# Rotary partners by DMA and in-place rotation inside the last recurrent head, convolution spread out, in a two-layer hybrid trunk

## Chip, core and metric

One NeuronCore of a Trainium2 chip runs the whole program. The metric is the device time of one execution, in microseconds (us).

## What is computed

Two layers over 288 tokens (256 of a new prompt, 8 times 4 of running samples). Each layer projects the normalised input to 40 tiles of 128 columns, feeds three mixers from them (windowed attention with sinks, HGRN2 recurrence, short gated convolution), projects their outputs back, and adds a SwiGLU block. The change is about the rotary embedding of queries and keys and about when the convolution runs:

```python
def partial_rope(x, pos):          # the first 16 of 64 dimensions of a head
    x1, x2 = xr[..., :half], xr[..., half:]                     # half = 8
    rot = jnp.concatenate([x1 * cos - x2 * sin, x2 * cos + x1 * sin], axis=-1)
    return jnp.concatenate([rot, x[..., ROT_DIM:]], axis=-1)

def short_conv(u, buf, w):         # u = cc * ch; the result is multiplied by cb
    up = jnp.concatenate([buf, u], axis=1)
    y = w[0] * up[:, 0:L] + w[1] * up[:, 1:1 + L] + w[2] * up[:, 2:2 + L]
```

The first eight dimensions of a head and the next eight are each other's partners. Row `d` of a tile needs its own value times cos plus its partner's value times sin with a sign.

## The kernel before

**Layout.** Features lie on the 128 partitions, tokens on the free axis. All weights stream from HBM as 754 slabs of 512 KB. SP loads a slab into one of four buffers `raw`, ACT rounds it (`hi`, L417, `whi`), DVE makes the remainder (`lo`, L712, `wlo`), and PE multiplies with both (L1459 to L1461: `whi` with the high and the low part of the activations, `wlo` with the high part). One slab is 2 tiles by 4 chunks by 3, that is 24 matmuls of 128x288. ACT and DVE work two slabs ahead of PE (`LEAD`); a buffer comes free when PE is through with its slab.

**Fill-in work.** The mixers run in the gaps of this stream. On each engine a mixer is a Python generator; after each slab (on PE in the recurrent heads after each half slab) every engine takes the generator's next step and runs on to the next `yield`. So the order of each engine's queue is set by where the `yield`s stand, and an engine that waits inside a step holds up the slabs behind it.

**Order of a layer.** The projection makes the tiles of the recurrence first (0 to 15: `HQ`, `HF`, `HI`, `HG`), then queries (16 to 23, `Q0`), keys and values (24, 25 and 26, 27, `KV`), and last the convolution's (28 to 39, `CB`, `CC`, `CH`). Four recurrent heads (`hgrn`, 8 slabs each) fill the time while tiles 16 to 31 are made, so tiles 16 to 27 are ready at the end of the third head. Then come two halves of attention (`attn`, `gg` = 0 and 1), 16 slabs each: `gg` = 0 beside the last projection slabs, `gg` = 1 beside the first half of the output projection. `conv` runs beside `gg` = 1; the second half of the output projection waits for its end (`half_b`).

**Head 3 on DVE.** Its generator ends with: `near` (the last masked copy, L829), a step in which heads 0 to 2 open the next head and head 3 does nothing, `sample_state(0)` (L898, waits for PE's `out`), then reciprocal, scaling and gating of the output (L905, L907, L911, after ACT's square root), `sample_state(1)` (L898), and the remainder `ml` (L916, after ACT's `mh`, L491). `hgrn_over` makes an engine wait for the ends of all these before it starts attention.

**Rotary before.** At the head of each half PE multiplies five tiles (one key tile, four query tiles) by a signed permutation, `partners` (L1602: four after the first slab, one after the second). DVE multiplies by sin (L973), POOL multiplies the tile by cos (L1349), DVE adds (L977) into `krg` or `qg`. ACT makes `krx`, the key tile with its halves swapped (L543, L544), and copies the sample queries to `qs` (L552). PE's first scores, `score(0)` (L1614), come after the third slab. POOL also copies the values (`vst_a`, L1351). `conv` starts at its sixth step and takes one piece per step to its thirteenth.

## Time and profile before

| | |
|---|---|
| median of 3 runs | 2590.35 us (2590.34 to 2590.42) |
| the profiled execution's own time | 2590.64 us |
| its span in the trace | 2588.9 us, 51434 instructions |
| TensorE | 99% busy, 19400 matmuls |
| VectorE, ScalarE, GpSimd | 57%, 39%, 14% busy |
| DMA | 419.97 MB, mean 162 GB/s |

The span runs from the first to the last recorded instruction; the execution's own time has 1.7 us around it. Busy times of matmuls overlap, because they are pipelined: the distance of two starts tells what one costs. In a timeline row the columns are start, duration, engine, line, operation, tiles and count, and in brackets the engine's idle time before it with what ended it.

### The profile page before, as it was taken

What the parts mean: (1) busy time and instruction counts of PE and PEld (TensorE: products, weight loads), DVE (VectorE), ACT (ScalarE), POOL (GpSimd) and SP (SyncE); (2) the same over time, 40 slices, a digit from 0 to 9 for tenths busy, and PEclk for the clock granted to TensorE, in tenths of its full rate; (3) what the DMA queues carried; (4) which work ended last, traced back from release to release, by engine and by line L of the source; (5) the groups of instructions that cost most, each with busy time, mean ns of one, the idle gap of its engine ahead of it and who ended that gap; (6) DMA issues with size and microseconds to landing.
All of it is one profiled execution on the core that took longest, in us unless ns stands there. A gap on an engine that the chain in (4) does not pass through costs nothing.

```text
span 2588.9 us, 51434 instructions
## 1 busy us (share of the span) xinstructions
PE 2558.7 (99%) x19400; PEld 2519.2 (97%) x19400; DVE 1483.5 (57%) x2055; ACT 1013.7 (39%) x1401; POOL 349.8 (14%) x290
## 2 busy tenths in 40 slices
PE   8999999999999999999999999999999999999997
PEld 8999999999999999999999999999999999999997
DVE  5576797555544445555545767875555444555455
ACT  5344554333333333333334544543333333333333
POOL 2001113111110011111100121031111000111111
PEclk9999999999999999999999999999999999999998
DMA  6544444444445444544454544445454455444443
GB/s 223 164 153 163 159 143 146 166 166 163 168 164 170 164 164 161 168 162 163 162 163 163 174 150 142 145 155 178 161 171 159 165 163 161 162 162 162 170 163 126
DMA packets 115724, 419.97 MB, mean 162 GB/s; under 512 B 13376, under 2 KB 14656, under 8 KB 115584
## 3 DMA queue, kind: packets, MB, share of 16 engines
q1 hardware_dynamic: 109152, 397.72, 45.9%
q0 software_dynamic: 3472, 14.04, 1.5%
q10 hardware_dynamic: 3024, 7.16, 0.7%
q8 instruction: 52, 0.85, 0.1%
q14 instruction: 24, 0.20, 0.0%
HBM read 411.06 MB, written 11.87 MB: 163 GB/s over the span
## 4 chain that ended last, share of the span: by engine, by line
PE 97%; DVE 1%; POOL 1%; ACT 0%; issue 0%; DMA 0%; SPq 0%; DVEq 0%; POOLq 0%; ACTq 0%
PE gp L1459 31%; PE gp L1461 30%; PE gp L1460 30%; PE mb L1503 1%; PE mb L1614 1%; PE mb L1635 0%; PE mb L1627 0%; POOL acc L1387 0%; PE mb L1602 0%; PE mb L1573 0%; DVE rstd L737 0%; DVE wlo L712 0%; DMA raw<-wstream 0%; PE mb L1512 0%; DVE x L1262 0%
## 5 line engine op out<-in xcount | busy, mean ns | idle before, releaser
L1459 PE MATMUL gp<-xh,whi 128*128 128x288 f32 x4096 | 1225.7, 299 | 12.6 <-DVE xl L1147 9.7
L1460 PE MATMUL gp<-xl,whi 128*128 128x288 f32 x4096 | 1209.7, 295 | 0.0
L1461 PE MATMUL gp<-xh,wlo 128*128 128x288 f32 x4096 | 1205.7, 294 | 0.0
L712 DVE TENSOR_TENSOR wlo<-raw,whi 128x1024 fp32r<-128x1024 f32 x754 | 970.9, 1321 | 336.4 <-ACT whi L417 332.5
L417 ACT ACTIVATE whi<-raw 128x1024 fp32r<-128x1024 f32 x754 | 769.1, 1052 | 572.3 <-PE gp L1461 541.9
L1459 PEld LDWEIGHTS gp<-xh,whi 128*128 128x128 f32 x4096 | 769.1, 188 | 24.7 <-issue 23.6
L1461 PEld LDWEIGHTS gp<-xh,wlo 128*128 128x128 f32 x4096 | 772.4, 189 | 0.0
L1460 PEld LDWEIGHTS gp<-xl,whi 128*128 128x128 f32 x4096 | 770.5, 188 | 0.8
L1459 PE MATMUL gp<-fh,whi 128*128 128x288 f32 x1408 | 416.7, 296 | 0.0
L1460 PE MATMUL gp<-fl,whi 128*128 128x288 f32 x1408 | 415.4, 295 | 0.0
L1461 PE MATMUL gp<-fh,wlo 128*128 128x288 f32 x1408 | 414.0, 294 | 0.0
L1461 PEld LDWEIGHTS gp<-fh,wlo 128*128 128x128 f32 x1408 | 265.2, 188 | 0.0
L1460 PEld LDWEIGHTS gp<-fl,whi 128*128 128x128 f32 x1408 | 264.3, 188 | 0.0
L1459 PEld LDWEIGHTS gp<-fh,whi 128*128 128x128 f32 x1408 | 263.8, 187 | 0.0
L1419 POOL TENSOR_TENSOR gw<-gb,gs 128x576 f32<-128x576 f32 x44 | 63.3, 1439 | 1246.1 <-ACT gs L604 1246.1
L608 ACT ACTIVATE fh<-fa 128x576 f32 (+1 forms) x44 | 30.2, 685 | 284.8 <-DVE fa L1111 284.8
L1111 DVE TENSOR_TENSOR fa<-gp,gw 128x288 f32<-128x288 f32 x88 | 36.2, 453 | 177.7 <-PE gp L1461 177.7
L1105 DVE TENSOR_TENSOR gb<-gp,rstd 128x288 f32<-128x288 f32 x88 | 36.2, 452 | 171.7 <-PE gp L1461 171.4
L604 ACT ACTIVATE gs<-gb 128x576 f32<-128x576 f32 x44 | 30.2, 686 | 263.6 <-DVE gb L1105 263.6
L752 DVE TENSOR_TENSOR x<-gp,x 128x288 f32 (+1 forms) x128 | 52.3, 450 | 138.4 <-PE gp L1461 138.3
L1421 POOL TENSOR_TENSOR gw<-gw,rstd 128x576 f32<-128x576 f32 x44 | 100.9, 2293 | 3.4
L424 ACT ACTIVATE xh<-x,par x64 | 30.8, 529 | 167.5 <-DVE x L752 167.5
(251 smaller groups left out, 1881.7 us busy)
## 6 DMA issues: line engine op xcount, KB each, us to landing
raw<-wstream SPq DMA_DIRECT2D x754, 512.0 KB, 4.2
s<-s_cache POOLq DMA_DIRECT2D x8, 512.0 KB, 9.7
hs_out<-s ACTq DMA_DIRECT2D x8, 512.0 KB, 2.8
caches_out<-caches POOLq DMA_DIRECT2D x8, 496.0 KB, 7.8
x<-x_in ACTq DMA_DIRECT2D x4, 576.0 KB, 8.5
y_out<-x SPq DMA_DIRECT2D x4, 576.0 KB, 2.8
kct<-kt_cache POOLq DMA_DIRECT2D x4, 512.0 KB, 6.3
vct<-v_cache POOLq DMA_DIRECT2D x4, 512.0 KB, 7.2
```

Of the source, the lines that this page charges most:

```text
L417: a.activation(whi[slot][:], raw[slot][:], ACT.Copy).then_inc(hi_ready, 1)
L424: m = a.activation(xh[:, bass.ds(2 * j + c, 1), :], x[:, bass.ds(2 * j + c, 1), :], ACT.Copy, scale=pcol(P_GAIN, tn * KC + 2 * j + c))
L604: a.activation(gs[:], gb[:], ACT.Sigmoid).then_inc(sig_ready, 1)
L712: v.tensor_tensor(wlo[slot][:], raw[slot][:], whi[slot][:].bitcast(F32), ALU.subtract).then_inc(lo_ready, 1)
L752: m = v.tensor_tensor(xc, gp[2 * bank + c][:, 0:TOK], xc, ALU.add)
L1105: m = v.tensor_tensor(gb[:, c, :], gp[c][:, 0:TOK], rstd[:], ALU.mult)
L1111: m = v.tensor_tensor(fa[:, c, :], gp[2 + c][:, 0:TOK], gw[:, c, :], ALU.mult)
L1419: e.tensor_tensor(gw[:], gb[:], gs[:], ALU.mult).then_inc(gw_steps, 1)
L1421: e.tensor_tensor(gw[:], gw[:], rstd[:].unsqueeze(1).to_broadcast([P, 2, TOK]), ALU.mult).then_inc(gw_steps, 1)
L1459: t.matmul(out, w_hi, mv_hi, start=first, stop=False)
L1460: t.matmul(out, w_hi, mv_lo, start=False, stop=False)
L1461: mm = t.matmul(out, w_lo, mv_hi, start=False, stop=last)
```

## The change

- **POOL**, after the recurrent heads, issues four DMAs (`rotary_partners`) that copy the partner rows of tiles 16 to 27, 8 partitions each, into rows of tiles that heads 0 to 2 are through with (`partner`, tiles 0 to 2, 4 to 6, 8 to 10, 12 to 14). Its cos products, the copy of the values and their waits go; the stores read `pj` itself.
- **DVE**, in head 3's empty step, multiplies all ten partner tiles by a signed sin and all ten tiles by cos in place (`rotary_products`: 2592, 288 and 2880 elements a partition). Behind `sample_state(0)` it adds the two (`rotary_sum`: 2592 and 288). This serves both halves. The sign is put into sin once, at the start.
- **PE** loses the `partners` matmuls. `score(0)` moves from the third step of a half to the first, and all that follows moves up by two steps.
- **ACT** makes `krx` in the first step instead of the second; the copies to `qs` move behind the first `turned`.
- **conv** on DVE takes its pieces at steps 2, 4, 6, 8, 10, 12 and 14 instead of 6 to 11 and 13; its buffers move out of the way of the hidden tiles.

```diff
-ROPE_ORDER = (4, 0, 1, 2, 3)
+ROTATED = KV + 2 - Q0
...
+        rot_sign = sb("rot_sign", [P, 1])
...
-        over = [wide[0] + size([P, Q0, TOK]), wide[0] + size([P, CB, TOK])]
+        over = [wide[0] + size([P, HI + 3, TOK]), wide[0] + size([P, HG, TOK])]
+        krx = sub(over, "krx", [P, TOK])
...
+        assert tail[1] == temp[0]
+        over = [tail[0], temp[1]]
+        up = sub(over, "up", [P, 4, UPW])
+        yc = sub(over, "yc", [P, 4, UPW - 2])
+        t = [over[0], temp[1]]
...
+        partner = pj[:, 0:Q0, :].rearrange("p (a b) t -> p a b t", b=4)[:, :, 0:3, :]
...
-                for _ in range(6):
+                for _ in range(3):
...
-                for _ in range(5):
+                for _ in range(9):
...
+                a.wait_ge(rv.sem, rv.at(l, "rot"))
+                a.activation(krx[0:64, :], pj[64:128, KV + gg, :], ACT.Copy)
+                a.activation(krx[64:128, :], pj[0:64, KV + gg, :], ACT.Copy).then_inc(aa.sem, aa.step("krx"))
...
                 for u in range(3):
                     turned(u)
+                    if u == 0:
+                        queries()
                     yield
...
+                    v.tensor_reduce(rot_sign[:], rot, AX.X, ALU.add)
...
+                    v.tensor_scalar(sin, sin, rot_sign[:, 0:1], -1.0, ALU.mult, ALU.mult)
...
+            def rotary_products(l):
+
+                v.wait_ge(group_out, attn_in(l))
+                v.wait_ge(partners_loaded, l * 64 + 64)
+                v.tensor_tensor(partner[:, 0:3], partner[:, 0:3], sin.unsqueeze(1).unsqueeze(1).to_broadcast([P, 3, 3, TOK]),
+                                ALU.mult)
+                v.tensor_tensor(partner[:, 3, 0, :], partner[:, 3, 0, :], sin, ALU.mult).then_inc(rv.sem, rv.step("sin"))
+                v.tensor_tensor(pj[:, Q0:Q0 + ROTATED, :], pj[:, Q0:Q0 + ROTATED, :],
+                                cos.unsqueeze(1).to_broadcast([P, ROTATED, TOK]), ALU.mult).then_inc(rv.sem, rv.step("cos"))
+
+            def rotary_sum(l):
+                v.wait_ge(rv.sem, rv.at(l, "cos"))
+                nine = pj[:, Q0:Q0 + 9, :].rearrange("p (a b) t -> p a b t", b=3)
+                v.tensor_tensor(nine, nine, partner[:, 0:3], ALU.add)
+                v.tensor_tensor(pj[:, Q0 + 9, :], pj[:, Q0 + 9, :], partner[:, 3, 0, :], ALU.add
+                                ).then_inc(rv.sem, rv.step("rot"))
...
                 if not last:
                     opening(T + 1, h + 1)
+                else:
+                    rotary_products(l)
                 yield
...
                 sample_state(0, "ssa", 1)
+                if last:
+                    rotary_sum(l)
                 yield
...
-                for _ in range(5):
-                    yield
-
-                v.wait_ge(at.sem, at.at(T * 2 + 1, "R3"))
-                v.wait_ge(ap_.sem, ap_.at(T * 2 + 1, "vst"))
+                yield
+                v.wait_ge(group_out, conv_in(T))
...
-                for n in ROPE_ORDER[:4]:
-                    rope(n)
-                yield
-                rope(ROPE_ORDER[4])
...
+            def rotary_partners(l):
+
+                T = l * HG_HEADS + HG_HEADS - 1
+                e.wait_ge(group_out, attn_in(l))
+                e.wait_ge(ho.sem, ho.at(T, "q"))
+                e.wait_ge(hs.sem, hs.at(T, "sig_g"))
+                e.wait_ge(hp.sem, hp.at(T, "gate"))
+                apart(e)
+                rows, half = pj[:, Q0:CB, :].rearrange("p (a b) t -> p a b t", b=3), ROT_DIM // 2
+                for head in (0, HEAD_DIM):
+                    for to, of in ((head, head + half), (head + half, head)):
+                        e.dma_start(partner[to:to + half], rows[of:of + half]).then_inc(partners_loaded, 16)
...
-                for k, n in enumerate(ROPE_ORDER):
-                    if k >= 2:
-                        e.wait_ge(av.sem, av.at(T, f"rot{ROPE_ORDER[k - 2]}"))
-                    tile = 4 * gg + Q0 + n if n < 4 else gg + KV
-                    apart(e)
-                    e.tensor_tensor(rt_a[:, k % 2, :], pj[:, bass.ds(tile, 1), :].rearrange("p o t -> p (o t)"), cos,
-                                    ALU.mult).then_inc(ap_.sem, ap_.step(f"cos{n}"))
-                e.tensor_copy(vst_a[:], pj[:, bass.ds(gg + (KV + 2), 1), :].rearrange("p o t -> p (o t)")
-                              ).then_inc(ap_.sem, ap_.step("vst"))
...
-                e.wait_ge(av.sem, av.at(T, f"rot{ROPE_ORDER[-1]}"))
+                e.wait_ge(rv.sem, rv.at(l, "rot"))
...
                     hgrn(l * HG_HEADS + h, h, l)
+                rotary_partners(l)
                 for gg in range(2):
...
-                    t.wait_ge(av.sem, av.at(T, f"sc{u - 1}" if u else "rot3"))
-                    if u == 0:
+                    if u:
+                        t.wait_ge(av.sem, av.at(T, f"sc{u - 1}"))
+                    else:
+                        t.wait_ge(rv.sem, rv.at(l, "rot"))
...
-                            keys = krg if i == u // 2 else krx
-                            mm = t.matmul(mb[i][:, m_ * P:(2 * m_ + 1) * P], qg[rows, u, m_ * P:(m_ + 1) * P],
+                            keys = pj[:, KV + gg, :] if i == u // 2 else krx
+                            mm = t.matmul(mb[i][:, m_ * P:(2 * m_ + 1) * P], pj[rows, Q0 + 4 * gg + u, m_ * P:(m_ + 1) * P],
...
-                for n in ROPE_ORDER[:4]:
-                    partners(n)
-                yield
-                t.wait_ge(av.sem, av.at(T, f"sin{ROPE_ORDER[0]}"))
-                partners(ROPE_ORDER[4])
-                yield
                 score(0)```

VectorE's queue from the end of `near` in head 3 to the end of the head, before the change (`wlo` is a slab's remainder, `s` the sample state, `pj` the projected tiles):

```order
L829 COPY_PREDICATED AT<-half_mask_60,mb 128x2x4x16
L712 TENSOR_TENSOR wlo_85<-raw_77,whi_81 128x1024
L898 SCALAR_TENSOR_TENSOR s_118<-s_118,tot,mb 128x128 x4
L712 TENSOR_TENSOR wlo_82<-raw_74,whi_78 128x1024
L905 RECIPROCAL osq<-osq 128x288
L907 SCALAR_TENSOR_TENSOR osb<-osb,par,osq 128x288
L911 TENSOR_TENSOR osb<-osb,gate 128x288
L898 SCALAR_TENSOR_TENSOR s_118<-s_118,tot,mb 128x128 x4
L712 TENSOR_TENSOR wlo_83<-raw_75,whi_79 128x1024
L916 TENSOR_TENSOR ml<-osb,mh 128x288
```

The same piece of VectorE's queue with the change:

```order
L849 COPY_PREDICATED AT<-half_mask_61,mb 128x2x4x16
L713 TENSOR_TENSOR wlo_86<-raw_78,whi_82 128x1024
L786 TENSOR_TENSOR pj<-pj,cst 128x3x864
L788 TENSOR_TENSOR pj<-pj,cst 128x288
L789 TENSOR_TENSOR pj<-pj,cst 128x2880
L920 SCALAR_TENSOR_TENSOR s_116<-s_116,tot,mb 128x128 x4
L795 TENSOR_TENSOR pj<-pj 128x2592
L796 TENSOR_TENSOR pj<-pj 128x288
L713 TENSOR_TENSOR wlo_83<-raw_75,whi_79 128x1024
L929 RECIPROCAL osq<-osq 128x288
L931 SCALAR_TENSOR_TENSOR osb<-osb,par,osq 128x288
L935 TENSOR_TENSOR osb<-osb,gate 128x288
```

The three products stand ahead of the state update, the two sums between it and the remainder of the first slab of attention; the reciprocal and all behind it follow.

ScalarE's queue from the head's end to the first steps of attention, before the change:

```order
L491 ACTIVATE mh<-osb 128x288 [waits hgrn_vector]
L494 DMA hp_out<-s_117 128x128 [waits hgrn_scalar]
L496 DMA hs_out<-s_118 128x1024 [waits hgrn_vector]
L417 ACTIVATE whi_80<-raw_76 128x1024 [waits slab_used,raw_ready2]
L417 ACTIVATE whi_81<-raw_77 128x1024 [waits hgrn_gpsimd,hgrn_sigmoids,hgrn_tensor,hgrn_scalar,hgrn_opening,hgrn_vector,slab_used,raw_ready3,attn_vector]
L543 ACTIVATE krx<-krg 64x288 [waits attn_vector]
```

and with the change:

```order
L490 ACTIVATE mh<-osb 128x288 [waits hgrn_vector]
L493 DMA hp_out<-s_115 128x128 [waits hgrn_scalar]
L495 DMA hs_out<-s_116 128x1024 [waits hgrn_vector]
L416 ACTIVATE whi_81<-raw_77 128x1024 [waits slab_used,raw_ready2]
L552 ACTIVATE krx<-pj 64x288 [waits hgrn_gpsimd,hgrn_sigmoids,hgrn_tensor,hgrn_scalar,hgrn_opening,hgrn_vector,rotary_vector,attn_vector]
L553 ACTIVATE krx<-pj 64x288
```

The swapped key tile is now made ahead of the second `whi` of attention, straight behind the wait for the whole recurrence.

## Rows read from the trace of the kernel before

**Rows 1.** List of PE's waits, whole span (engine, line, releaser: us, times, longest).
```profile
PE gp L1459 <- DVE xl L1147: 9.7, 1, 9.7
PE mb L1493 <- POOL acc L1288: 3.9, 1, 3.9
PE gp L1459 <- DVE wlo L712: 2.3, 4, 0.8
PE mb L1614 <- DVE qg L977: 0.8, 2, 0.4
```

**Rows 2.** PE's timeline around the first four partner matmuls of layer 0.
```profile
254.71 0.30 PE L1460 MATMUL gp<-xl,whi 128*128 128x288 f32 x1
...
260.84 0.29 PE L1461 MATMUL gp<-xh,wlo 128*128 128x288 f32 x1
260.98 2.10 PE L1602 MATMUL mb<-pj,cst 128*128 128x288 f32 x8
...
263.05 0.30 PE L1460 MATMUL gp<-xl,whi 128*128 128x288 f32 x1
```

**Rows 3.** PE's groups of instructions by shape (count, busy us, mean ns).
```profile
L1602 PE MATMUL mb<-pj,cst 128*128 128x288 f32 x40 | 11.0, 405 | 0.0
```

**Rows 4.** DVE's timeline at the end of head 3 of layer 0.
```profile
242.39 1.22 DVE L712 TENSOR_TENSOR wlo<-raw,whi 128x1024 fp32r<-128x1024 f32 x1
252.61 1.12 DVE L898 SCALAR_TENSOR_TENSOR s<-s,tot,mb 128x128 f32<-128x128 f32 x4 [9.00 <-PE mb L1582]
253.65 1.22 DVE L712 TENSOR_TENSOR wlo<-raw,whi 128x1024 fp32r<-128x1024 f32 x1
255.31 1.95 DVE L905 RECIPROCAL osq<-osq 128x288 f32<-128x288 f32 x1 [0.44 <-ACT osq L487]
...
259.26 1.22 DVE L712 TENSOR_TENSOR wlo<-raw,whi 128x1024 fp32r<-128x1024 f32 x1
260.40 0.45 DVE L916 TENSOR_TENSOR ml<-osb,mh 128x288 fp32r<-128x288 f32 x1
```

**Rows 5.** The same timeline in layer 1, the state update of head 3.
```profile
1530.20 1.12 DVE L898 SCALAR_TENSOR_TENSOR s<-s,tot,mb 128x128 f32<-128x128 f32 x4 [9.01 <-PE mb L1582]
```

**Rows 6.** DVE's groups by shape, window of the second half, layer 0.
```profile
L964 DVE TENSOR_TENSOR al<-pj,ah 128x1152 fp32r<-128x1152 f32 x1 | 1.4, 1354 | 0.0
```

**Rows 7.** POOL's timeline in head 3 of layer 0.
```profile
229.38 0.55 POOL L1303 DMA_DIRECT2D s<-s_cache  x1
...
232.69 2.28 POOL L1314 TENSOR_TENSOR vm<-vks,own 96x512 f32<-96x512 f32 x1 [1.11 <-ACT vks L448]
```

**Rows 8.** The profile's DMA queue and DMA issues (count, KB each, us to landing).
```profile
q1 hardware_dynamic: 109152, 397.72, 45.9%
...
s<-s_cache POOLq DMA_DIRECT2D x8, 512.0 KB, 9.7
...
cv_out<-cnew POOLq DMA_DIRECT2D x2, 36.0 KB, 2.8
```

**Rows 9.** ACT's timeline at the start of attention, layer 0.
```profile
259.83 2.27 ACT L417 ACTIVATE whi<-raw 128x1024 fp32r<-128x1024 f32 x2 [0.95 <-DVE s L898]
264.20 0.44 ACT L543 ACTIVATE krx<-krg 64x288 f32<-64x288 f32 x1 [2.11 <-DVE krg L977]
264.66 0.44 ACT L544 ACTIVATE krx<-krg 64x288 f32<-64x288 f32 x1
```

**Rows 10.** PE's timeline at the span's start and end.
```profile
9.68 0.58 PE L1459 MATMUL gp<-xh,whi 128*128 128x288 f32 x1 [9.68 <-DVE xl L1147]
...
15.82 0.32 PE L1460 MATMUL gp<-xl,whi 128*128 128x288 f32 x1
...
2569.58 0.29 PE L1461 MATMUL gp<-fh,wlo 128*128 128x288 f32 x1
2573.81 1.33 PE L1493 MATMUL mb<-acc,mean_x 128*128 128x288 f32 x2 [3.94 <-POOL acc L1288]
```

**Rows 11.** Busy time in the stretch 2572 to 2573 (PE, PEld, DVE, ACT, POOL, granted clock, DMA share, GB/s).
```profile
2572.00:2573.00 1.00, 0.00 (x0) 0.00 (x0) 0.68 (x1) 0.98 (x2) 0.92 (x2) 0.72 0.00 0
```

More of the change, by code:

```diff
@@ L535, in turned, with queries @@
                     m.then_inc(aa.sem, aa.step(f"pT{u}"))
+                def queries():
+                    a.wait_ge(ap_.sem, ap_.at(T, "qs0"))
+                    for g in range(2):
+                        for i in range(4):
+                            half = 64 * (i % 2)
+                            at_ = 16 * g + DEC_SEQ * i
+                            m = a.activation(qs[64 * g:64 * g + 64, :, at_:at_ + DEC_SEQ], pj[half:half + 64, Q0 + 4 * gg + 2 * g + i // 2, SEQ:TOK]
+                                             .rearrange("p (b t) -> p b t", t=DEC_SEQ), ACT.Copy)
+                    m.then_inc(aa.sem, aa.step("qs"))
                 def out_hi(u):
@@ L1597, in attn @@
                 t.wait_ge(aa.sem, aa.before(T))
-                def partners(n):
-                    tile = 4 * gg + Q0 + n if n < 4 else gg + KV
-                    t.matmul(mb[ROPE_ORDER.index(n) % 4][:, 0:TOK], rot, pj[:, bass.ds(tile, 1), :].rearrange("p o t -> p (o t)"),
-                             start=True, stop=True).then_inc(at.sem, at.step(f"R{n}"))
                 def score(u):
-                    t.wait_ge(av.sem, av.at(T, f"sc{u - 1}" if u else "rot3"))
-                    if u == 0:
+                    if u:
+                        t.wait_ge(av.sem, av.at(T, f"sc{u - 1}"))
+                    else:
+                        t.wait_ge(rv.sem, rv.at(l, "rot"))
                         t.wait_ge(aa.sem, aa.at(T, "krx"))
@@ L1673, in attn @@
                                 at_ = 2 * P + r * SAMP
-                                mm = t.matmul(mb[0][rows, at_:at_ + SAMP], qs[:, b, :], krg[:, SEQ:TOK],
+                                mm = t.matmul(mb[0][rows, at_:at_ + SAMP], qs[:, b, :], pj[:, KV + gg, SEQ:TOK],
                                               start=True, stop=True)
```

77 lines of the change are left out of this document (22 added, 55 removed), and 1 row of the table av.

## The prediction

> **What bounds the kernel now.** I began with the list of PE's waits, since PE is busy for nearly the whole span: PE waits about 17 us in 2588.9, and 13.6 of them lie at the program's two ends, where this change does nothing [rows 1]. So time is gained only by taking instructions off PE or by ending one of its few waits, and it is lost wherever a new wait opens. In the part that changes, the list has one entry: the first scores of an attention half wait for DVE's rotated queries, 0.8 us in two pieces of 0.4 [rows 1]. Then I read PE's timeline where the permutation matmuls stand, for what one costs between its neighbours [rows 2], and last the queues of DVE, POOL and ACT around the end of head 3, because the work goes there [rows 4, 7, 9].
>
> **What comes off PE.** The neighbours of the first four permutation matmuls are 47 matmuls of the stream whose first and last start 6.13 us apart, so one costs 6.13 / 46 = 0.133 us [rows 2]. From the start of the last of them at 260.84 to the start of the second matmul behind the permutations at 263.05 there are 2.21 us, where two steps of 0.133 would stand: four permutations cost 2.21 - 0.27 = 1.94 us, or 0.485 each. The trace has 40 records for them, two for each (8 records for these four) [rows 2, 3]: 20 matmuls, 20 x 0.485 = **9.7 us**. Nothing covers them, PE being the bound. The old wait before the scores, **0.8 us**, goes with them.
>
> **Three products on DVE.** Two rows give the price by size: 288 elements take 0.45 us [rows 4], 1152 take 1.354 [rows 6], so 1.046 ns an element. 2592 elements come to 2.86 us and 2880 to 3.16; an instruction starts some 0.08 before the one ahead of it ends (a remainder of 1.22 us begins 1.14 before its follower, [rows 4]). The products take 2.78 + 0.37 + 3.08 = 6.2 us. They are covered: DVE is idle for 9.0 us, from 243.6 until PE's `out` releases the state update at 252.6, in layer 1 as well [rows 4, 5]. They end at 249.8 with 2.8 us to spare. If that cover were gone, each us would go to the chain below.
>
> **The four DMAs.** POOL ends head 3's last product at 234.97 and has nothing else; an issue takes 0.55 [rows 7], so the last is out at 237.2. How long an SBUF-to-SBUF copy of 8 partitions takes, the trace doesn't show. Bounds: 2.8 us, a 36 KB store alone on the queue, and 9.7 us, a 512 KB load behind another [rows 8]; 108 KB four times lies between, and I take 6, landing at 243.2, just before DVE asks. What lands before 246.4 costs nothing. At the upper end, 246.9, it is 0.5 us a layer.
>
> **The two sums on DVE, the costly part.** They stand behind the state update and ahead of the first remainder of attention: 2.78 + 0.37 = 3.15 us, where DVE has no idle time to speak of. Followed through the old rows: the remainder starts at 253.65 + 3.15 = 256.8 and ends at 258.0. PE wants it at 257.8 (24 steps of 0.133 before 260.98, [rows 2]), so PE waits **0.3 us**. The reciprocal starts at 257.9 instead of 255.31 (it had waited 0.44 for ACT), 2.6 later, and `ml` ends at 260.85 + 2.6 = 263.5 [rows 4]. What waits for `ml`: ACT, before it swaps the key tile. Its store waits for the second state update and its next `whi` starts at 259.83 + 2.6 = 262.4, ending at 263.5 [rows 9]; then the two half copies, 0.46 + 0.44, so `krx` is there at 264.5. And PE now asks for its first scores after one slab, not three. That slab starts 0.3 late, at 258.1, and PE is at the scores at 261.35. **A new wait of 264.55 - 261.35 = 3.2 us**, in each layer. The second half's scores need only a key swap ahead of which the first half has ended two steps sooner: no wait.
>
> Bounds of this wait: if the sums took half as long, the remainder would be in time and the wait 1.6; if they took twice as long, it would be 6.3 and the remainder 3.4 late. I take the row's price, since the operands are of the same kind.
>
> **The rest.** POOL loses its cos products and the copy of the values, which PE never waited for. The copies to `qs` move behind the first transposes and delay the second exponentials; PE's list has no wait for any exponential so far [rows 1], and if their slack were too short, it would show there. The convolution issues the same instructions, spread out; no entry of PE's list names any of them, before or at its end [rows 1], so it is worth nothing, and if DVE fell behind there it would show as a wait of the third or fourth transposes, tenths of a us. The sign of sin costs two small DVE instructions once, ahead of remainders; all of PE's waits for remainders are four, 2.3 us [rows 1], and two such instructions could add some 0.5.
>
> **The sum.** -9.7 - 0.8 + 2 x 0.3 + 2 x 3.2 = -3.5 us against the profiled execution (2590.64, that is the span of 2588.9 and 1.7 around it). The median of the runs is 0.3 lower; from it, 2586.85.
>
> **The clock.** One cost remains that the sum leaves out. When PE stands still long enough, its granted clock falls. After the last stream matmul (started 2569.58) PE had nothing to do, and the stretch 2572 to 2573 has a mean of 0.72 granted, that is a fall from 2.4 to 1.2 GHz at about 2572.4, 2.5 us into the standstill [rows 10, 11]. At the start, after 9.7 us without work, 25 matmuls stand 0.24 us apart, from 9.68 to 15.82, where 0.133 would do [rows 10]: 6.14 - 3.33 = 2.8 us lost. A new wait of 3.2 us is longer than the 2.5 and may set off the same. Bounds: nothing, or 2.8 in both layers, 5.6. I take 2.0, one fall of a shorter kind, since the standstill is a third as long as that at the start. Then the time is 2590.35 - 3.5 + 2.0 = **2588.8**.
>
> The Trainium skill has a rule that speaks against this change: in "TensorE: Matmul & The Clock Gate", section "Why this matters for your kernels", idle gaps between bursts of matmuls are to be avoided because an idle stretch brings the array back to half rate. The trace agrees that it happens, with the fall at 2572.4. By that rule in full the kernel would take 2592.4, without it 2586.85.
>
> **Rivals.**
> 1. *The new wait is short or absent* (0.20). For it: the chain runs through four engines' queues, and a guess of 0.5 us too much at three places brings the wait to 1.7; the stated price of the sums could be too high. Against: in the changed order of ACT, `krx` waits for the whole recurrence. Without the wait -9.7 - 0.8 + 0.6 = -9.9, 2580.4; with 1.6 us and no late remainder 2583.0.
> 2. *The partners come late and DVE stands in its queue for them* (0.08). All of DVE's later work, `out`'s consumers and the remainders, is behind that wait. A copy touches only 8 partitions, so its rows may go to few of the 16 DMA engines. The stream's packets took 0.459 x 16 x 2588.9 / 109152 = 0.174 us each at 3.6 KB [rows 8]. The partners are 128 runs of 3.4 KB, some 21 us on one engine, 2.7 on eight. On one they land near 259, 12.7 us late, twice: 2586.85 + 25.4 = **2612**, slower. It decides from a landing at 248.2 on (the gain of 3.5 is gone), and over 0.2% from 250.8. For it: no row shows such a copy. Against: 512 KB take 9.7 us even behind another load.
> 3. *The clock falls in both layers and stays down long, and the wait is a little longer than 3.2* (0.12): 2592.4 to 2597.
> 4. That the change does not do what it says: PE's changed list has no permutation left, so this can't be more than a trifle.
>
> **How the numbers follow.** A run tells about 0.2%, 5.2 us, from no change: faster means under 2585.2, slower over 2595.5. My forecast, a wait of 2.4 to 4 us with no, one or two falls of the clock, has 0.60 and lies between 2585.5 and 2593, inside the bound. Rival 1 (0.20) gives faster, and 0.02 of the forecast's lower edge too. Rival 2 (0.08) is mostly slower; half of rival 3 (0.06) is. So faster 0.22, same 0.65, slower 0.13. For 8 in 10 the range takes the forecast, the upper half of rival 1 and most of rival 3: 2582.5 to 2595.
>
> **What would show it.** PE's wait list should have the first scores (L1619) twice, near 3.2 us, released by ACT's `krx`, and the first remainder of attention for 0.3; no row of permutations; the sums at 2.8 us each layer, right behind the state update; DVE's idle time before that update down to about 2.8 us. If the granted clock falls, matmuls behind the wait stand 0.24 us apart. The prediction is wrong if the scores wait under 1 us, if the products wait for the DMAs beyond 246.4, or if PE waits in the second half of attention, where the spread convolution stands.

## The result, and the profile after

| | |
|---|---|
| before, median | 2590.35 us |
| changed, median of 20 runs | **2596.24 us** (2588.53 to 2600.11) |
| ratio to before | 1.0019, 95% interval 1.0012 to 1.0025 |
| forecast | 2588.8 us, range 2582.5 to 2595.0 |

The change made the kernel 5.9 us slower, and its median lies 1.2 us above the upper end of the range. The scatter is new too: the runs of the kernel before lie within 0.9 us, those of the changed kernel over 11.6 us. The profiled execution happened to be the fastest of them, 2588.53 us. Its list of TensorE's (PE's) waits (engine, line, what ended the wait: us, times, longest):

```profile
PE gp L1468 <- DVE xl L1157: 9.6, 1, 9.6
PE mb L1619 <- ACT krx L553: 6.1, 2, 3.1
PE mb L1502 <- POOL acc L1298: 3.9, 1, 3.9
PE gp L1468 <- DVE wlo L713: 2.4, 5, 0.8
...
PE mb L1575 <- ACT vks L471: 0.4, 1, 0.4
```

Beside [rows 1] the wait of the scores for the rotated queries (0.8) is gone, and the new wait of the first scores for `krx` is there: 6.1 us in two pieces. The last row is new too, and it is the small end of what cost most. The same kernel's PE timeline at the standstill:

```profile
257.34 0.29 PE L1470 MATMUL gp<-xh,wlo 128*128 128x288 f32 x1
257.86 0.37 PE L1468 MATMUL gp<-xh,whi 128*128 128x288 f32 x1 [0.23 <-DVE wlo L713]
...
260.99 0.29 PE L1470 MATMUL gp<-xh,wlo 128*128 128x288 f32 x1
264.35 0.55 PE L1619 MATMUL mb<-pj 64*128 64x128 f32 x1 [3.07 <-ACT krx L553]
...
266.34 0.44 PE L1469 MATMUL gp<-xl,whi 128*128 128x288 f32 x1
266.58 0.44 PE L1470 MATMUL gp<-xh,wlo 128*128 128x288 f32 x1
```

No matmul starts between 260.99 and 264.35; behind it the stream's matmuls stand 0.24 us apart instead of 0.133. The granted clock had fallen to 1.2 GHz: over 264 to 268 its mean is 0.57 (stretch; busy time of PE, PEld, DVE, ACT, POOL, then granted clock, DMA share, GB/s), while the same place of layer 1 shows no fall behind the same standstill.

```profile
264.00:268.00 4.00, 3.65 (x18) 3.03 (x19) 2.83 (x5) 2.55 (x3) 3.12 (x7) 0.57 0.83 279
...
1542.00:1546.00 4.00, 4.00 (x32) 3.67 (x33) 3.45 (x9) 2.38 (x3) 3.52 (x7) 1.00 0.88 293
```

A mean of 0.57 over 4 us is 4 x 0.43 / 0.5 = 3.4 us at 1.2 GHz, at most 1.7 us lost. DVE's timeline beside [rows 4]:

```profile
244.75 2.86 DVE L786 TENSOR_TENSOR pj<-pj,cst 128x2592 f32<-128x2592 f32 x1 [0.21 <-DMA pj<-pj]
...
247.90 3.15 DVE L789 TENSOR_TENSOR pj<-pj,cst 128x2880 f32<-128x2880 f32 x1
252.31 1.12 DVE L920 SCALAR_TENSOR_TENSOR s<-s,tot,mb 128x128 f32<-128x128 f32 x4 [1.27 <-PE mb L1591]
253.35 2.85 DVE L795 TENSOR_TENSOR pj<-pj 128x2592 f32<-128x2592 f32 x1
256.12 0.45 DVE L796 TENSOR_TENSOR pj<-pj 128x288 f32<-128x288 f32 x1
256.49 1.22 DVE L713 TENSOR_TENSOR wlo<-raw,whi 128x1024 fp32r<-128x1024 f32 x1
257.63 1.94 DVE L929 RECIPROCAL osq<-osq 128x288 f32<-128x288 f32 x1
```

Sums, late remainder and reciprocal stand where the prediction put them, within 0.4 us. The products start 1.2 us later than it said (244.75 in place of 243.6, the last 0.2 for the DMAs) and end with 1.27 us to spare in place of 2.8. What the prediction left out is ScalarE's (ACT's) queue a little earlier. First the kernel before, then the changed one, from `whi` to the copies of the turned keys (`vks`), for which PE's next state product waits:

```profile
239.13 1.06 ACT L417 ACTIVATE whi<-raw 128x1024 fp32r<-128x1024 f32 x1 [5.93 <-DMA raw<-wstream]
240.70 1.06 ACT L417 ACTIVATE whi<-raw 128x1024 fp32r<-128x1024 f32 x1 [0.52 <-DMA raw<-wstream]
243.09 1.06 ACT L417 ACTIVATE whi<-raw 128x1024 fp32r<-128x1024 f32 x1 [1.32 <-PE gp L1461]
...
246.06 0.27 ACT L472 ACTIVATE vks<-mb 96x128 f32<-96x128 f32 x1
```

```profile
237.94 1.06 ACT L416 ACTIVATE whi<-raw 128x1024 fp32r<-128x1024 f32 x1 [5.69 <-DMA raw<-wstream]
242.23 1.06 ACT L416 ACTIVATE whi<-raw 128x1024 fp32r<-128x1024 f32 x1 [3.23 <-DMA raw<-wstream]
245.08 1.06 ACT L416 ACTIVATE whi<-raw 128x1024 fp32r<-128x1024 f32 x1 [1.79 <-DMA raw<-wstream]
...
247.07 0.27 ACT L471 ACTIVATE vks<-mb 96x128 f32<-96x128 f32 x1
```

In the kernel before, ACT already waited for DMA ahead of two of the three slabs, and ahead of the third for PE alone. In the changed kernel it waits for DMA ahead of all three, the third starts 2 us later, and the key copies stand behind it in ACT's queue. The DMA view of 229 to 246 (issues: count, KB each, median us to landing) has the reason; again before, then changed:

```profile
raw<-wstream SPq DMA_DIRECT2D x6, 512.0 KB, 7.0
```

```profile
raw<-wstream SPq DMA_DIRECT2D x5, 512.0 KB, 9.7
pj<-pj POOLq DMA_DIRECT2D x4, 108.0 KB, 6.0
```

The partner copies themselves land after 6.0 us in the median, the value I had taken. But the weight slabs beside them land after 9.7 us instead of 7.0.

### The profile page after: what moved, and what is told of

Same layout as the page of the kernel before. It is cut to its first block and busy times, and to the rows that moved or that the text cites. A ratio compares the mean times of both kernels' runs of the same rounds, so it can differ in the third digit from the quotient of the medians.

```text
span 2586.9 us, 51267 instructions
## 1 busy us (share of the span) xinstructions
PE 2550.8 (99%) x19360; PEld 2512.3 (97%) x19360; DVE 1483.0 (57%) x2027; ACT 1012.0 (39%) x1401; POOL 327.2 (13%) x274
## 3 DMA queue, kind: packets, MB, share of 16 engines
q1 hardware_dynamic: 109152, 397.72, 46.2%
## 5 line engine op out<-in xcount | busy, mean ns | idle before, releaser
L1468 PE MATMUL gp<-xh,whi 128*128 128x288 f32 x4096 | 1225.4, 299 | 12.6 <-DVE xl L1157 9.6
L1469 PE MATMUL gp<-xl,whi 128*128 128x288 f32 x4096 | 1209.8, 295 | 0.0
L1470 PE MATMUL gp<-xh,wlo 128*128 128x288 f32 x4096 | 1205.7, 294 | 0.0
L713 DVE TENSOR_TENSOR wlo<-raw,whi 128x1024 fp32r<-128x1024 f32 x754 | 969.6, 1320 | 338.4 <-ACT whi L416 334.6
L416 ACT ACTIVATE whi<-raw 128x1024 fp32r<-128x1024 f32 x754 | 769.0, 1052 | 584.3 <-PE gp L1470 545.0
L1468 PEld LDWEIGHTS gp<-xh,whi 128*128 128x128 f32 x4096 | 769.2, 188 | 25.2 <-issue 24.3
L1470 PEld LDWEIGHTS gp<-xh,wlo 128*128 128x128 f32 x4096 | 772.5, 189 | 0.0
L1469 PEld LDWEIGHTS gp<-xl,whi 128*128 128x128 f32 x4096 | 770.6, 188 | 0.6
L1468 PE MATMUL gp<-fh,whi 128*128 128x288 f32 x1408 | 416.7, 296 | 0.0
L1469 PE MATMUL gp<-fl,whi 128*128 128x288 f32 x1408 | 415.4, 295 | 0.0
L1470 PE MATMUL gp<-fh,wlo 128*128 128x288 f32 x1408 | 414.0, 294 | 0.0
L1470 PEld LDWEIGHTS gp<-fh,wlo 128*128 128x128 f32 x1408 | 265.2, 188 | 0.0
L1469 PEld LDWEIGHTS gp<-fl,whi 128*128 128x128 f32 x1408 | 264.3, 188 | 0.0
L1468 PEld LDWEIGHTS gp<-fh,whi 128*128 128x128 f32 x1408 | 263.8, 187 | 0.0
## 6 DMA issues: line engine op xcount, KB each, us to landing
raw<-wstream SPq DMA_DIRECT2D x754, 512.0 KB, 4.2
s<-s_cache POOLq DMA_DIRECT2D x8, 512.0 KB, 9.7
hs_out<-s ACTq DMA_DIRECT2D x8, 512.0 KB, 2.8
kct<-kt_cache POOLq DMA_DIRECT2D x4, 512.0 KB, 4.9
vct<-v_cache POOLq DMA_DIRECT2D x4, 512.0 KB, 6.4
```

The costliest lines, as they stand in the source:

```text
L416: a.activation(whi[slot][:], raw[slot][:], ACT.Copy).then_inc(hi_ready, 1)
L713: v.tensor_tensor(wlo[slot][:], raw[slot][:], whi[slot][:].bitcast(F32), ALU.subtract).then_inc(lo_ready, 1)
L1468: t.matmul(out, w_hi, mv_hi, start=first, stop=False)
L1469: t.matmul(out, w_hi, mv_lo, start=False, stop=False)
L1470: mm = t.matmul(out, w_lo, mv_hi, start=False, stop=last)
```

## The experiments

The lines ahead of each result are what was put down before the run. All medians are of 5 to 11 executions; those of the kernel before on the same chips were 2590.3 to 2590.6. In kernels with an edit the line numbers stand a few lines off.

**The same kernel again.** No edit.

> The changed kernel once more, for a second profiled execution. Its 20 runs lay between 2588.5 and 2600.1 us, far wider than the 0.9 us of the kernel before, and the profiled one was the fastest. Theory A (clock): TensorE stands still for about 3.3 us before the first scores of each layer, the granted clock falls after some of these standstills and not after others, and each fall costs several us because it stays at 1.2 GHz longer than the 3.4 us that the fastest run shows. So a slower execution shows one or two longer stretches at 1.2 GHz that begin just behind the standstills (near 264 and 1541 us), and its excess over 2588 us is about half of their length; the wait itself stays at 3.1 us. Theory B (transfers): the partners land at another time in each execution, so a slower execution shows the wait before the first scores itself longer, by the excess, with the vector engine waiting for the transfers. Theory C (second half): the excess lies in waits behind 265 us that the spread convolution makes. Median 2594 to 2598 us by all three.

Measured 2596.0 us (2590.08 to 2603.4). The profiled execution took 2591.35 and shows both things: the score wait unchanged at 2 x 3.1, a mean clock below one behind both standstills (3.4 us at 1.2 GHz each), and a wait for the key copies of 2.0 us:

```profile
PE mb L1619 <- ACT krx L553: 6.1, 2, 3.1
...
PE mb L1575 <- ACT vks L471: 2.0, 2, 1.3
```

Theory B as I had put it (partners late, score wait longer) has nothing for it: that wait is 6.1 in both profiles of this kernel. Neither profile is of one of the longer executions, though.

**Filling the wait.** In `attn` on PE, `gg` = 0:

```diff
-                    t.wait_ge(hv.sem, hv.last(l * HG_HEADS + HG_HEADS, "ssb"))
                     t.wait_ge(ha.sem, ha.last(l * HG_HEADS + HG_HEADS, "root"))
+                    for _ in range(6):
+                        t.matmul(mb[3][:, 0:TOK], rot, cos, start=True, stop=True)
+                    t.wait_ge(hv.sem, hv.last(l * HG_HEADS + HG_HEADS, "ssb"))
```

> Only edit: six products of the rotation matrix with the cosines (128x288 floats, about 0.49 us each, 2.9 us together, into a bank that is read by nobody) run on TensorE in the wait before the first scores of each layer. The wait for the rotated tiles is then nearly as long as before but the engine works in it. Theory A: the granted clock does not fall there, so the runs draw together to within about 1 us and the median is about 2587 us (the sum without the clock, 2586.85). Theories B and C: the spread stays 8 to 12 us wide and the median stays at 2595 to 2597 us.

Measured 2593.11 us (2587.71 to 2596.88). That is 2.9 us less with useless work in the wait. With scatters of 13 and 9 us this pair alone doesn't prove A; the same pair without copies, further down, does (3.6 us, scatters of 2.4 and 1.2). The spread stayed at 9 us and the median 6 us above A's 2587, so A is not all. The profiled execution has no fall of the clock behind the score place and waits 2.7 us at L1575 in one layer.

**Attention two slabs later.** Two empty steps (`if gg == 0: yield; yield`) ahead of the first scores on PE and DVE and behind `krx` on ACT; on PE:

```diff
+                if gg == 0:
+                    for _ in range(2):
+                        yield
                 score(0)
                 yield
```

> Only edit: in the first half the attention of all three engines starts two slabs later (two empty steps ahead of the first scores on TensorE, VectorE and ScalarE), as it stood in the kernel before. The rotated tiles are ready when the scores come. Theory A: no standstill, so no fall of the clock: 2586.85 less the 6.4 us of the two waits, about 2580.5 us, runs within 1 us of each other. Theory B: the transfers land as late as before but nobody waits for them so soon: about 2580.5 us too, but VectorE still waits for them in some executions. Theory C: the spread of 8 to 12 us stays, about 2590 us.

Measured 2590.74 us (2588.62 to 2595.41). The score wait is gone and 5.3 us are gained, where A and B gave 15. Two rows of PE's waits say what took its place:

```profile
PE gp L1474 <- DVE wlo L716: 6.4, 8, 1.7
...
PE mb L1581 <- ACT vks L471: 2.3, 2, 1.7
```

DVE's sums stand ahead of remainders, and without the score wait PE stands for such a remainder, 1.7 us in each layer; and the key copies are late here too. So one wait was hidden behind the other. Behind the wait of 1.7 us for the key copies, in layer 0, the clock fell as well: its mean over 250 to 262 is 0.86, that is 12 x 0.14 / 0.5 = 3.4 us at 1.2 GHz.

**Half the sums.** `rotary_sum(l, 0)` adds the five tiles of the first half in head 3; `rotary_sum(l, 1)` the other five in attention, behind `out_lo(0)`; the second half's users wait for the second sum.

```diff
-                v.tensor_tensor(nine, nine, partner[:, 0:3], ALU.add)
...
+                for to, p in (((0, 3), partner[:, 0]), ((3, 4), partner[:, 1, 0:1]), ((8, 9), partner[:, 2, 2:3])
+                              ) if gg == 0 else (((4, 6), partner[:, 1, 1:3]), ((6, 8), partner[:, 2, 0:2]),
+                                                 ((9, 10), partner[:, 3, 0:1])):
+                    tiles = pj[:, Q0 + to[0]:Q0 + to[1], :]
+                    m = v.tensor_tensor(tiles, tiles, p, ALU.add)
+                m.then_inc(rv.sem, rv.step("rot1" if gg else "rot"))
```

> Only edit: the sum of the rotary products is made for the five tiles of the first half in the last recurrent head (about 1.65 us in place of 3.3) and for the other five tiles four steps later, in the attention of the first half. The wait before the first scores gets shorter by about 1.65 us, to some 1.5 us. Theory A: the standstill is half as long, the clock falls seldom or not at all: 2586.85 less 3.3, about 2583.5 us, spread within 2 us. Theories B and C: less by 3.3 us only, median 2592 to 2594 us and the spread as wide as before.

Measured 2593.95 us (2591.39 to 2597.91): 2.1 us less than the changed kernel, which the scatter of both could make by itself, and the score wait is 4.2 in place of 6.1: the wait's own share came back and little else. The spread is 6.5 us (13.3 in the run of the same kernel again), not the 2 of theory A. PE's timeline of layer 1 shows the other standstill at its longest:

```profile
1523.26 0.29 PE L1477 MATMUL gp<-xh,wlo 128*128 128x288 f32 x1
1526.50 0.80 PE L1582 MATMUL mb<-vk 128*128 128x128 f32 x2 [2.94 <-ACT vks L471]
```

And the stretch behind it:

```profile
1526.00:1533.00 7.00, 6.50 (x22) 4.75 (x23) 4.28 (x3) 1.83 (x6) 0.00 (x0) 0.52 0.14 56
```

PE stands 2.9 us for ACT's key copies, and the clock is down over nearly all of the next 7 us (mean 0.52). This led to theory D: the copies crowd the DMA engines in head 3, a slab is late, ACT stands for it with the key copies behind, PE stands, and the clock may fall there as well.

**No copies.** In `rotary_partners`:

```diff
-                for head in (0, HEAD_DIM):
-                    for to, of in ((head, head + half), (head + half, head)):
-                        e.dma_start(partner[to:to + half], rows[of:of + half]).then_inc(partners_loaded, 16)
+                e.sem_inc(partners_loaded, 64)
```

> Only edit: the four partner copies by DMA are left out, so the partners are whatever the tiles held and the scores come out other than the reference's; every product, sum and wait on the engines stays. The last four runs showed a second standstill that the changed kernel's first profile has only as 0.7 us: TensorE waits 0.7 to 3.2 us in head 3 for ScalarE's copies of the keys (L1575 in the changed kernel), because ScalarE stands for a late weight slab ahead of them, while the DMA engines are 85 to 95% busy (71 and 49% before). Theory D (crowding): the four copies, 432 KB beside the 512 KB state load, the 496 KB cache shift and the weight stream, delay that slab. It expects L1575 to vanish from the waits, the score wait to stay at 2 x 3.1 us, and the median to fall from 2596.0 to about 2590 us (2586.85 and a clock fall of 1.7 us behind each score wait), spread 2 to 5 us. Theory A alone (all of it is the clock behind the score wait): the median stays at 2595 to 2597 us.

The kernel leaves the partner values out, so only its time is read. Measured 2590.15 us (2588.68 to 2591.08): 5.9 us less than the changed kernel, spread 2.4 us. The waits:

```profile
PE mb L1616 <- ACT krx L553: 6.1, 2, 3.1
```

The whole list has no row for the key copies any more. The clock fell behind both score waits, behind the second for longer (8 x 0.43 / 0.5 = 6.9 us at 1.2 GHz):

```profile
264.00:269.00 5.00, 4.42 (x23) 3.80 (x24) 3.80 (x10) 2.77 (x3) 3.55 (x7) 0.66 0.85 283
1541.00:1549.00 8.00, 6.99 (x34) 6.37 (x35) 5.77 (x14) 5.16 (x13) 3.56 (x7) 0.57 0.85 310
```

**No copies and the wait filled.** Both edits.

> Both edits together: no partner copies (the scores come out other than the reference's), and the six products that keep TensorE at work in the wait before the first scores. If A and D are both true, nothing is left that varies: about 2586.9 us, spread within 1.5 us, no stretch at 1.2 GHz but that at the end. If something third is at work (the spread convolution, theory C), it stays above 2589 us or spreads.

Measured **2586.59 us** (2585.57 to 2586.80). With both causes away the time is the prediction's sum, 2586.85, within 0.3 us. That leaves no room for a third cause of more than some tenths, unless two more cancel.

**All cache shifts moved.** The `caches_out` copy, which moves 496 KB from memory to memory in each head (the cache shift), leaves the heads; each step of `squares` in the second half of the output projection issues half of one.

```diff
                     squares(l * 2 + 1, j)
+                    rows = bass.ds(2 * j + l * HG_HEADS * CACHE_PART, CACHE_PART // 2)
+                    e.dma_start(caches_out[rows], caches[rows, DEC_SEQ:, :]).then_inc(cache_moved, 16)
```

> Only edit: the cache shift, a 496 KB copy from memory to memory in every recurrent head, is taken out of the heads and issued as eight pieces of 248 KB per layer in the second output projection; the partner copies stay. Theory D: with one of the three large transfers away, the weight slab in head 3 is late by less than 0.5 us, L1575 goes from the waits or falls below 0.5 us, and the time is that of the run without copies, about 2590 us, spread 2 to 5 us. If the crowding is by the state load or by the copies' own small rows: waits of L1575 stay at 1 to 3 us and the median at 2594 to 2596 us.

Measured 2590.22 us (2589.49 to 2590.97), the time without copies, with the copies in place; no row for the key copies.

**The version of all three.** Later attention, half sums, shift moved.

> A version meant to be faster: the attention of the first half starts two slabs later, the sums are split in two halves, and the cache shift is moved out of the heads. By A and D together no standstill over 1 us is left: 2586.85 less 6.4 for the score waits and less 0.6 for the late remainder, 2580 to 2582 us, spread within 2 us. If weight slabs or VectorE's remainders are late elsewhere, 2585 us or more.

Measured 2581.88 us (2581.08 to 2582.20), ratio to before 0.9967 (0.9955 to 0.9979).

**One more edit for it.** In head 3 on DVE:

```diff
+                if last:
+                    yield
                 sample_state(1, "ssb", 2)
```

> The fastest run so far (2581.88 us) with one edit more: in head 3 the second state update on VectorE comes one step later, behind the remainder that TensorE still waits 0.8 us for in each layer (gap of 0.96 us between its matmuls at 260.71 and 1534.03). Expected: those two gaps go, 2 x 0.8 us, about 2580.3 us; if what waits for the state update (the store, and ScalarE's next slab behind it) is late instead, no gain, 2581.5 to 2582.5 us.

Measured 2581.94 us (2581.06 to 2587.29): no gain. The gap is still there, 0.92 us (260.02 to 260.94) in place of 0.96.

**Without the half sums.**

> The changed kernel with two of the three edits of the fastest run: attention two slabs later and the cache shift moved, but the sums in one piece. By the account so far the remainders behind the sums are then late as in the run with the later attention alone (a gap of 1.94 us in each layer where the fastest run has 0.96), so 2581.88 + 2 x 1.0 = about 2583.9 us, within 2 us of spread. If the halved sums are what matters most, 2586 us or more; if they don't matter, 2582 us.

Measured 2585.0 us (2584.06 to 2589.27). Seven of 11 executions lie at 2584.06 to 2585.02, near the 2583.9 expected, and the two gaps in the profile are the 1.94 us that were expected (260.56 to 262.51, 1535.33 to 1537.27). Four executions at 2587.6 to 2589.3 do not fit.

**Convolution back at its old steps**, in the version of all three: five empty steps ahead of its first piece on DVE and one between pieces, as in the kernel before (on ACT 6 and 5 in place of 3 and 9).

> The fastest run so far with the convolution back to the steps it had in the kernel before (first instruction at the sixth step in place of the second, one step between instructions in place of two). Nothing waited for the convolution in any profile, so the time is the same within the runs' scatter: 2581.9 us, 2581 to 2583. Theory C, by which the spread of the convolution costs or gains something: a change of over 1 us, and new waits between 300 and 350 us.

Measured 2580.69 us (2580.31 to 2580.97). That is 1.2 us less than the version of all three, more than expected; about a third of it is the spread. Before the fourth transposes PE stood 0.35 us from the last stream matmul's start with the convolution spread, and 0.14 with it back (both from PE's timeline, layer 0; first spread, then back):

```profile
361.68 0.29 PE L1483 MATMUL gp<-mh,wlo 128*128 128x288 f32 x1
362.03 0.55 PE L1645 MATMUL mb<-cst,sc 128*128 128x128 f32 x3
```

```profile
361.01 0.30 PE L1480 MATMUL gp<-mh,wlo 128*128 128x288 f32 x1
361.15 0.60 PE L1642 MATMUL mb<-cst,sc 128*128 128x128 f32 x4
```

That is 0.2 us in each layer (0.34 and 0.13 in layer 1). The two profiles were 0.7 us apart before attention began (first matmul behind the sums' gap at 261.67 and 260.98), which this edit can't have done.

**The cache shift moved in the kernel before.**

> The kernel before, with the cache shift moved out of the recurrent heads as in the other runs and nothing else. In the kernel before no wait of TensorE lies in the heads, so room on the DMA engines there is worth nothing: the same as before, 2590.3 us within 0.5. If it is faster by several us, the gain of the fastest run would come from the moved shift and not from the rotary change.

Measured 2591.19 us (2590.43 to 2596.84). So the gain of the fast versions doesn't come from the moved shift; on the contrary. Five of the 11 executions took 2593.6 to 2596.8, and the profiled one (2596.55) waits for remainders at the start of the SwiGLU block, 3.4 us at the longest (0.8 in the kernel before, [rows 1]):

```profile
PE gp L1459 <- DVE wlo L712: 7.1, 5, 3.4
```

ACT stands 7.6 us for a slab there (454.3 to 461.9), and the DMA view of 448 to 470 shows slabs landing after 11.1 us beside a piece of the shift, where the kernel before has 4.3:

```profile
raw<-wstream SPq DMA_DIRECT2D x5, 512.0 KB, 11.1
caches_out<-caches POOLq DMA_DIRECT2D x1, 248.0 KB, 10.5
```

So the shift took the late slabs with it. It needs no full engines for that: the mean DMA share of 455 to 472 is 0.34. Which part of the transfer path holds the slab back is not shown by any run here. The four late executions of the run without the half sums, and two of the run with the later state update, may be of the same kind; no profile shows one of them. All these eleven were on one chip, where the kernel before stayed under 2591.1; two kernels with the shift in the output projection had none in 17 executions on another chip, and the one with the convolution back had none in five on this one. So how often it happens is open.

**Only head 3's shift, 20 us later.** In the changed kernel, head 3 leaves out `caches_out` at its old place and issues it behind the partner copies, after PE's `out`:

```diff
+                e.wait_ge(ht.sem, ht.at(T, "out"))
+                apart(e)
+                rows = bass.ds(T * CACHE_PART, CACHE_PART)
+                e.dma_start(caches_out[rows], caches[rows, DEC_SEQ:, :]).then_inc(cache_moved, 16)
```

> The changed kernel with one edit: only the cache shift of head 3 moves, by some 20 us, from ahead of the partner copies to behind the head's output products (about 252 us), where the DMA engines carried nothing in the profiles; those of heads 0 to 2 stay. Theory D, crowding at that moment: the same as with all shifts moved: no wait of L1575 over 0.5 us, two score waits of 3.1 us, about 2590.2 us with a spread of 2 us, and no slower executions, since nothing is added to the output projections. If it is the sum of the traffic in the heads, or the number of transfers ahead on the issuing queue, that counts: L1575 stays at 1 us or more and the median at 2592 to 2596 us. If the shift now delays the slabs of attention: new waits between 257 and 275 us.

Measured 2589.3 us (2588.10 to 2590.38). The number and the bytes of transfers are those of the changed kernel; only the moment differs. ACT's queue now reads as follows: every slab is there before PE frees a place, and the key copies are where they were before the change.

```profile
239.31 1.06 ACT L416 ACTIVATE whi<-raw 128x1024 fp32r<-128x1024 f32 x1 [2.58 <-PE gp L1476]
242.96 1.06 ACT L416 ACTIVATE whi<-raw 128x1024 fp32r<-128x1024 f32 x1 [2.59 <-PE gp L1476]
...
245.94 0.27 ACT L471 ACTIVATE vks<-mb 96x128 f32<-96x128 f32 x1
```

```profile
raw<-wstream SPq DMA_DIRECT2D x6, 512.0 KB, 4.2
pj<-pj POOLq DMA_DIRECT2D x4, 108.0 KB, 5.2
```

The second fence is the DMA view of 229 to 246: slabs land after 4.2 us instead of 9.7.

**The version that beats both kernels.** Later attention, half sums, convolution at its old steps, head 3's shift behind the head.

> The fastest run so far (2580.69 us: attention two slabs later, sums halved, convolution at its old steps), but with the shift of head 3 alone moved, behind the head's output products, in place of all shifts moved into the second output projection. Theory D: 2580.7 us, 2580 to 2582, and without the executions of 2586 to 2597 us that the runs with the shift in the output projection showed in part (4 of 11, 2 of 7, 5 of 11). If those are of another cause they are seen here too.

Measured **2581.15 us** (2580.88 to 2582.10), ratio to before 0.9964 (0.9951 to 0.9978): 9 us faster than the kernel before and 15 faster than the changed one, with no slow tail in its 5 executions, which are few to exclude one. It is no faster than the version with all shifts moved and the convolution back (2580.69).

## Why the prediction was wrong

The median of the changed kernel is put together from the runs like this:

| step | us | from |
|---|---|---|
| the prediction's sum, clock left out (2586.85) | 2586.6 | measured 2586.59, no copies and wait filled |
| clock behind the score waits | +3.6 | 2590.15 - 2586.59 (with the copies there: 2596.0 - 2593.1 = 2.9) |
| late slabs in head 3 | +5.9 | 2596.0 - 2590.15 (other ways: 2593.1 - 2586.6 = 6.5; 2596.0 - 2589.3 = 6.7) |
| changed kernel | 2596.0 | |

**What was right.** The 20 permutation matmuls at 0.485 (no run takes them alone, but the sum that holds them fits), the new score wait (3.2 forecast, 3.05 measured, with `krx` at 264.2 against 264.5), the late remainder (0.3 forecast, 0.39 more between two starts than the usual 0.133), the prices of products and sums (2.86, 3.15; sums 2.85 and 0.45), the covered products. The sum of these was off by 0.3 us, the convolution's 0.4 included. For the convolution the text had said that a DVE falling behind would show as tenths of a us at the third or fourth transposes: it is 0.2 a layer at the fourth.

**What was right by luck.** 6 us for the DMAs is the median of the four, but DVE waits for the last, and that one landed at about 244.6, some 10 us after its issue at 234.5. It was in time because POOL issued the first at 232.74, 2.2 us earlier than the prediction had it from the old rows. Two bounds of the score wait were wrong without consequence: with half the sums PE too comes 0.3 us earlier, so the wait is 1.9 and not 1.6 (2.1 measured with half the sums), and with sums twice as long PE would come as late as `krx`, so the wait would stay at 3.2 and not grow to 6.3.

**The step that failed** is "The four DMAs": "What lands before 246.4 costs nothing." It priced the copies by who waits for them, and asked only when they land. They landed in time and cost 5.9 us all the same, because of what they took from other transfers: the weight slabs due at the same moment. A row that hints at it was there to be read: in the kernel before the DMA engines carry the state load, the cache shift and the stream together, and from 230 to 235 their share is 0.99:

```profile
230.00:235.00 5.00, 5.00 (x41) 5.00 (x40) 4.56 (x12) 1.50 (x3) 3.85 (x2) 1.00 0.99 332
```

ACT's `whi` then waited for the stream at 239.13 and 240.70. The sign that tells most is how long the slabs took to land: 7.0 us from 229 to 246, where the median of all 754 is 4.2. The engines' share tells less than I thought. The runs put side by side, from 229 to 246:

| kernel | cache shift there | copies | slabs land after, us (median) | DMA share |
|---|---|---|---|---|
| before | yes | no | 7.0 | 0.69 |
| no copies | yes | no | 6.9 | 0.67 |
| changed | yes | yes | 9.7 | 0.90 |
| head 3's shift behind | no | yes | 4.2 | 0.86 |
| all shifts moved | no | yes | 3.9 | 0.85 |
| kernel before, shifts moved | no | no | 3.8 | 0.61 |

Rows of the fourth column for no copies, all shifts moved, and the kernel before with its shifts moved; then of the last for the kernel before and for head 3's shift behind:

```profile
raw<-wstream SPq DMA_DIRECT2D x6, 512.0 KB, 6.9
...
raw<-wstream SPq DMA_DIRECT2D x6, 512.0 KB, 3.9
...
raw<-wstream SPq DMA_DIRECT2D x6, 512.0 KB, 3.8
...
229.00:246.00 17.00, 17.00 (x146) 16.71 (x144) 12.26 (x32) 5.64 (x11) 4.84 (x4) 1.00 0.69 227
...
229.00:246.00 17.00, 17.00 (x146) 16.62 (x144) 15.18 (x33) 5.76 (x12) 4.04 (x6) 1.00 0.86 226
```

The copies made slabs late only beside the shift (9.7 to 12.9 us in the five profiles with both); without the shift they cost the slabs little (3.9 and 4.2 against 3.8), at a share of 0.85. The shift makes slabs late by itself (7.0 against 3.8), and the copies add to that. Rival 2 looked at the copies too, but put the standing engine at DVE, where the wait was 0.2 us (0.5 in layer 1); the engine that stood was ACT, in front of key copies that have nothing to do with rotation.

**The clock term** had the right mechanism and was too small: 2.0 taken, 3.6 measured, inside its bounds of 0 to 5.6. With that alone the time would have been 2590.4, inside the range. The late slabs also feed this term: a wait for the key copies can bring the clock down by itself (the one of 2.9 us with half the sums, the one of 1.7 with the later attention; not the one of 2.7 with the wait filled). The price of a fall can be read from the distance between the starts of the first and the second scores: 7.8 us without a fall (wait filled without copies, both layers; layer 1 of the changed kernel's first profile), 9.2 to 9.3 with 3.4 us at 1.2 GHz, 10.5 with 6.9. So the short fall cost 1.4 to 1.5 us and the long one 2.7. Single executions then add up from 2586.6, the wait at L1575 and their falls: 2586.6 + 0.4 + 1.4 = 2588.4 for the changed kernel's profiled one (2588.5 measured), 2586.6 + 2.0 + 3.0 = 2591.6 for the second (2591.4), 2586.6 + 2.7 = 2589.3 for the one with the wait filled (2589.6), 2586.6 + 1.5 + 2.7 = 2590.8 for the one without copies (2590.6). No profile is of the slowest execution, 2600.11. Its mean granted clock was 0.993 where the fastest had 0.996, and 0.003 x 2600 = 7.8 us, within 2.6 us for rounding, so a good part of its 11.6 us more may be clock; how many falls, and where, stays open. So does how the 5.9 us of the median divide into waiting for the key copies and falls of the clock behind that wait.

**The range** therefore missed for one cause that was not in it. No rival held a price for transfers that delay transfers; rivals 2 (up to 2612) and 3 (up to 2597) could reach 2596, both for other reasons. The prediction's signs of being wrong did not name this step either: the scores waited 3.05 us, the products did not wait beyond 246.4, and in the second half PE stood no more than the 0.2 us above.

The Trainium skill has the rule that I should have weighed, in "Trainium Kernel Development and Optimization", section "Key Constraints": DMAs issued from SP, ACT and POOL all run on the same 16 DMA engines and interleave. The runs agree that transfers of one queue slow those of another: with the shift there, the slabs on SP's queue land after 9.7 us with the copies on POOL's queue and after 6.9 without. But 4.2 us with the same copies and no shift shows that meeting on the engines is not enough to make them late.

## What to carry to other kernels

A transfer has two prices: who waits for it, and what it makes late. Before adding one beside a stream that is prefetched only two slabs deep, read in just that stretch how long the stream's own transfers take to land (7.0 us here, 4.2 over the whole span) and whether its consumers already wait for DMA there; neither the stream's 45.9% of the whole span [rows 8] nor the DMA share of the stretch tells it. Another transfer beside it may be the better one to move: putting one cache shift of each layer 20 us later brought back 6.7 us. And a new wait of a few us on TensorE costs more than its length: fill it, split what it waits for, or put the waiting step later, and look at the scatter of the runs as well as at the fastest profile, since a median 8 us above the best run is the sign of something that happens by chance.

## What the runs showed that was not expected

- **A standstill of 3.36 us between two matmuls' starts was followed by a fall of the clock 9 times in 10** (two layers each of the changed kernel's two profiles and of the runs without copies, with all shifts moved, and with head 3's shift behind): the only exception is layer 1 of the first. The price of one fall was 3.4 us at 1.2 GHz in seven, about twice that in the other two. With the half sums, where the standstill was 2.39 us, the clock fell once in two; behind the wait of 2.7 us in the kernel with the filled wait it didn't, behind the one of 1.7 us with the later attention it did. So the length of the wait alone did not decide.
- **Useless work made the kernel faster**: six matmuls nobody reads, in a wait that stays as long, gained 3.6 us without the copies (2.9 with them, where the scatter is wider than that).
- **A transfer from memory to memory that nobody waits for can cost several us where it is put**: with the shift in the output projection of the unchanged kernel, 5 of 11 executions were 3 to 6 us slower, on the one chip where this was run.
